# Filter generation and the later modulation products moved from the prologue into the first layer's input projection

## The chip, the cores and the metric

The kernel runs on one core of a Trainium2 chip. The metric is the device time of one execution in microseconds. Three runs of the kernel before gave a median of 3544.75 us (3544.44 to 3552.7). The engines are TensorE (PE; its weight loads are PEld), VectorE (DVE), ScalarE (ACT), GpSimd (POOL) and SyncE (SP, here the queue that issues most transfers).

## The reference

The reference is a two-layer backbone on 1024 latent and 256 context tokens of width 1024. This change touches only what stands before and in the input projection of layer 0:

```python
m_lat = jnp.split((s_lat @ ada_w[i] + ada_b[i])[:, None, :], 6, axis=-1)      # per layer, also with s_ctx
h_lat = modulate(rmsnorm(x_lat, norm1_g[i]), m_lat[0], m_lat[1])              # y * (1 + scale) + shift
u_lat = h_lat @ w_in                                                          # layer 0: 1536 + 384 + 256 + 32 columns

def hyena_filters(L, w1, b1, w2, b2, w3, freq):                               # L = 1024 and 256
    h = jnp.sin(freq * (z @ w1 + b1))
    h = jnp.sin(freq * (h @ w2 + b2))
    h = (h @ w3).reshape(L, HY_ORDER, D_HY)
    return jnp.transpose(h * window[:, None, :], (1, 0, 2))
# later: irfft(rfft(z) * rfft(h)), a long convolution with each of the two filters
```

`ada_w` has 2 x 1024 x 6144 values. Only the first 2048 columns of layer 0 (shift and scale of the first norm) are needed for the first norm.

## The kernel before

The program is a row of blocks; all engines meet at the end of each. The names and lines that matter:

`prologue` loads everything small, `x` (L581) and the constants. It computes the two hidden layers of the filter network (L597, L603) with the sine's argument reduced on VectorE (L650 to L656), the filter tiles of 128 positions by 512 channels (L613, windowed on VectorE at L665), a butterfly of the window's blocks (`butterfly_lat`, `butterfly_ctx`, L451 to L497) and the spectra by matmuls with a table (`forward`, L510 to L516), which ScalarE copies out (L714) and stores. ScalarE squares `x` (L704) and GpSimd adds the squares up in `ss` (L731). Between these, TensorE works through the modulation: class `Stream` loads 32 pieces of `ada_w` of 1.5 MB, each three tiles of 128 columns, into two buffers (L388, L392). For each piece, eight matmuls with 32 stationary columns go to four column groups of the array (L404), ScalarE copies the four partial rows (L421), three matmuls turn and sum them to columns (L410), and ScalarE stores those in `mods` (L424). At the end VectorE makes the coefficients of all four norms (`coefficients`, L433 to L442).

`even_in` begins with the first norm (`Norm`: column sums L307, root and reciprocal, broadcast L315, `rr` L346, `xr` L335, `h_hi` L355, `h_lo` L328) and then multiplies: 18 output tiles ("items") of 128 rows by 1280 tokens, two per weight pair, each with 8 k-tiles x 3 passes (high and low halves of weights and activations) x 3 token chunks. Items 0 and 1 are interleaved (`first_pair`, L273), the rest follow one another (`item`, L252). Per item ScalarE makes the high half of the next weights (L232) and the centre tap of the short convolution or a copy (L772, L785, L787), VectorE the low half (L238) and the outer taps (L802). Two accumulators, banks 0 to 2 and 3 to 5 of PSUM, alternate. The loops over items are hardware loops.

Each engine executes its own queue in order; semaphores order the engines against one another. Nothing else plans the order: it is as written.

Of the kernel before, what the change touches and what calls it, by code (L numbers as in the profile page):

```python
# [29 lines left out]
P = 128  # L30
D = 1024
KT = D // P
# [190 lines left out]
def full(use):  # L223

    return use + 2
# [65 lines left out]
class Norm:  # L291


    def __init__(self, k, n):
# [8 lines left out]
    def tensor(self, k, e):  # L303
        if k.sqs:
            e.wait_ge(k.ss_done, k.sqs)
        for j in range(self.tiles):
            mm = e.matmul(k.bank[:, 6, j:j + 1], k.ss[:, j * P:(j + 1) * P], k.ones[:, 0:1], start=True, stop=True)  # L307
# [11 lines left out]
    def vector(self, k, e):  # L319
        t = self.tiles  # L320
# [3 lines left out]
        e.reciprocal(k.rstd[:, 0:t], k.stat[:, 0:t]).then_inc(k.rstd_ready, 1)  # L324
        e.wait_ge(k.rr_ready, self.bcs + len(self.chunks))
# [14 lines left out]
    def scalar(self, k, e):  # L340
        t, n = self.tiles, self.n
        e.wait_ge(k.ms_ready, n + 1)
        e.activation(k.stat[:, 0:t], k.stat[:, 0:t], ACT.Sqrt).then_inc(k.sd_ready, 1)
        for c, (c0, m) in enumerate(self.chunks):
            e.wait_ge(k.bc_full, self.bcs + c + 1)
            e.activation(self.rr[:, c0:c0 + m], k.bank[:, 7 - c % 2, 0:m], ACT.Copy).then_inc(k.rr_ready, 1)  # L346
        for kk in range(KT):
# [13 lines left out]
ADA_M = 3  # L361
ADA_LOADS = 2 * 48 // ADA_M


class Stream:
# [5 lines left out]
    def __init__(self, k):  # L371
        words = KT * ADA_M * P
        assert H0 + 30080 + ADA_M * P <= END - words and words <= 4 * WS
        self.w = [k.at(f"ada_w{s}", at, [P, KT, ADA_M * P]) for s, at in enumerate((S0, END - words))]
        self.full = [k.sem(f"ada_landed{s}") for s in range(2)]
        self.sums = [k.sem(f"ada_sums{s}") for s in range(2)]
        self.read = [k.sem(f"ada_read{s}") for s in range(2)]
        self.stored = [k.sem(f"ada_stored{s}") for s in range(2)]
        self.columns = [k.sem(f"ada_columns{s}") for s in range(2)]
        self.row = [k.at(f"ada_row{s}", H0 + 28544 + s * ADA_M * P, [P, ADA_M * P]) for s in range(2)]  # L380
        self.group = [[k.bank[32 * j:32 * j + 32, 4 + s, 0:ADA_M * P] for j in range(4)] for s in range(2)]
        self.out = [k.bank[:, 4 + s, 0:ADA_M * P] for s in range(2)]
        self.turned = [k.bank[:, 4 + s, ADA_M * P:ADA_M * (P + 2)] for s in range(2)]
        self.made = self.copied = 0

    def load(self, k, e):
        for s in range(2):
            e.dma_start(self.w[s][:, :, :], k.d["ada_w"][s]).then_inc(self.full[s], 16)  # L388
        with e.Fori(0, ADA_LOADS // 2 - 1) as i:
            for s in range(2):  # L390
                e.wait_ge(self.sums[s], i + 1)
                e.dma_start(self.w[s][:, :, :], k.d["ada_w"][i * 2 + (s + 2)]).then_inc(self.full[s], 16)  # L392

    def products(self, k, e, count):

        with e.Fori(0, count) as n:
            i = n + self.made
            for s in range(2):
                e.wait_ge(self.full[s], i * 16 + 16)
                e.wait_ge(self.stored[s], i + 1)  # L400
                for half in range(2):
                    for j in range(4):
                        kk = 4 * half + j
                        mm = e.matmul(self.group[s][j], k.silu_c[:, 32 * kk:32 * kk + 32], self.w[s][:, kk, :],  # L404
                                      start=(half == 0), stop=(half == 1))
                mm.then_inc(self.sums[s], 1)
            for s in range(2):
# [20 lines left out]
    def coefficients(self, k, e, steps):  # L428
        for s in range(2):
            e.wait_ge(self.stored[s], ADA_LOADS // 2 + 1)  # L430
# [1788 lines left out]
```

## Time and profile before

| | |
|---|---|
| median of three runs | 3544.75 us |
| the profiled execution | 3543.79 us, its span 3542.1 us |
| TensorE busy | 3230.7 us, 91% of the span |
| VectorE, ScalarE, GpSimd busy | 1583.9, 969.9, 357.5 us |
| mean granted TensorE clock | 0.954 |
| loads of `ada_w` | 32 of 1536 KB, all in the first 260 us |
| loads of weight halves | 194 of 512 KB |

A timeline row gives the start, the time, the engine, the line, the operation and its operands, how many instructions are merged in it, and in brackets how long the engine stood before it and what ended that. A float32 matmul appears as two records on TensorE. A row of stretches gives the busy time of each engine in the stretch with its number of instructions, then the granted clock of TensorE (1.00 is 2.4 GHz, 0.50 is 1.2 GHz), the share of the DMA engines and GB/s.

### The profile page before, as it was taken

Reading aid. Unit: us, or ns where it says so; the run is one execution under the profiler, and the core shown is the slowest. Engines: PE = TensorE matmul, PEld = TensorE weight load, DVE = VectorE, ACT = ScalarE, POOL = GpSimd, SP = SyncE. Lnnn points to the kernel's source line nnn. Section 1 sums busy time; section 2 is a strip of 40 time slices with the busy share of each in tenths; the row PEclk is TensorE's granted clock in tenths of the full one; section 3 lists DMA queues with packets and bytes.
Section 4 is the critical chain, followed back from the end, with each engine's and each line's share of the span. In section 5 each row is a group of like instructions: output and inputs, shape, how many; then the busy total and the mean of one; then the engine's idle time right before and its main releaser. Section 6 shows DMA issues by size and latency. Waiting matters only on the chain. (4 is left out here: it accounts for less than half of the span.)

```text
span 3542.1 us, 37967 instructions
## 1 busy us (share of the span) xinstructions
PE 3230.7 (91%) x15170; PEld 2525.1 (71%) x15170; DVE 1583.9 (45%) x1846; ACT 969.9 (27%) x1105; POOL 357.5 (10%) x252
## 2 busy tenths in 40 slices
PE   5878998799965889999999999899988899999999
PEld 2337885455554678888888888777866788888887
DVE  5304316666578533333222322567775432332333
ACT  2224112344410223111111111377782411111111
POOL 3000000177722110000000000200001000000000
PEclk8878999799987999999999999899998999999999
DMA  6772210000211410111111111211103111111112
GB/s 239 284 277 94 80 50 3 0 1 1 116 56 42 154 36 30 36 37 37 41 36 36 39 40 36 80 30 38 36 29 111 49 48 48 47 47 47 47 48 76
DMA packets 45561, 228.95 MB, mean 65 GB/s; under 512 B 6377, under 2 KB 6761, under 8 KB 39179
## 3 DMA queue, kind: packets, MB, share of 16 engines
q1 hardware_dynamic: 41594, 203.37, 16.7%
q10 hardware_dynamic: 1728, 13.63, 0.9%
q0 software_dynamic: 2128, 10.36, 0.7%
q8 instruction: 84, 1.38, 0.2%
q14 instruction: 27, 0.21, 0.0%
HBM read 201.65 MB, written 25.69 MB: 64 GB/s over the span
## 5 line engine op out<-in xcount | busy, mean ns | idle before, releaser
L252 PE MATMUL bank<-h_hi,w_hi 128*128 128x512 f32 (+1 forms) x2616 | 702.7, 368 | 14.1 <-DVE h_lo L1645 7.2
L252 PE MATMUL bank<-h_lo,w_hi 128*128 128x512 f32 (+1 forms) x2616 | 700.5, 368 | 0.0
L252 PE MATMUL bank<-h_hi,w_lo 128*128 128x512 f32 (+1 forms) x2616 | 700.2, 367 | 0.0
L238 DVE TENSOR_TENSOR w_lo<-w_raw,w_hi 128x1024 fp32r<-128x1024 f32 x194 | 262.5, 1353 | 660.9 <-ACT w_hi L232 658.4
L252 PEld LDWEIGHTS bank<-h_hi,w_hi 128*128 128x128 f32 x2616 | 451.9, 188 | 99.5 <-issue 14.6
L252 PEld LDWEIGHTS bank<-h_lo,w_hi 128*128 128x128 f32 x2616 | 452.6, 188 | 88.1 <-issue 2.9
L252 PEld LDWEIGHTS bank<-h_hi,w_lo 128*128 128x128 f32 x2616 | 452.3, 188 | 85.1
L1577 DVE SCALAR_TENSOR_TENSOR x<-bank,c_mods,x 128x1024 f32<-128x1024 f32 (+3 forms) x280 | 271.7, 1005 | 256.5 <-PE bank L252 256.4
L232 ACT ACTIVATE w_hi<-w_raw 128x1024 fp32r<-128x1024 f32 x194 | 203.8, 1051 | 647.7 <-PE bank L252 608.9
L252 PE MATMUL bank<-hid_hi,w_hi 128*128 128x512 f32 (+1 forms) x880 | 242.9, 373 | 11.6 <-DVE x L1577 11.6
L252 PE MATMUL bank<-hid_hi,w_lo 128*128 128x512 f32 (+1 forms) x880 | 240.4, 371 | 0.0
L252 PE MATMUL bank<-hid_lo,w_hi 128*128 128x512 f32 (+1 forms) x880 | 240.4, 371 | 0.0
L1777 DVE TENSOR_TENSOR hid<-silu_gate,bank 128x1280 f32<-128x1280 f32 (+1 forms) x44 | 59.6, 1354 | 393.2 <-PE bank L252 390.8
L1744 ACT ACTIVATE hid_hi<-hid 128x1280 fp32r<-128x1280 f32 (+1 forms) x44 | 51.4, 1167 | 504.7 <-DVE hid L1777 504.7
L252 PEld LDWEIGHTS bank<-hid_hi,w_hi 128*128 128x128 f32 x880 | 153.2, 188 | 47.7 <-DVE x L1577 19.3
L1126 POOL TENSOR_TENSOR a_psum<-a_psum,probsT 128x512 f32<-128x512 f32 x128 | 174.2, 1371 | 28.5 <-ACT probsT L1322 26.9
L252 PEld LDWEIGHTS bank<-hid_hi,w_lo 128*128 128x128 f32 x880 | 154.0, 188 | 29.5
L252 PEld LDWEIGHTS bank<-hid_lo,w_hi 128*128 128x128 f32 x880 | 154.0, 188 | 29.5
L1740 ACT ACTIVATE silu_gate<-bank 128x1280 f32<-128x1280 f32 (+1 forms) x44 | 50.0, 1135 | 422.5 <-PE bank L252 422.5
L1595 POOL TENSOR_TENSOR ss<-ss,sq_ev 128x1280 f32<-128x1280 f32 x14 | 41.4, 2957 | 1027.5 <-ACT sq_ev L1586 1027.4
L1228 DVE TENSOR_REDUCE a_mx<-bank 128x1 fp32r<-128x1280 f32 (+1 forms) x80 | 101.2, 1269 | 90.9 <-PE bank L1141 90.8
L1322 ACT ACTIVATE probsT<-bank 128x512 f32<-128x512 f32 (+1 forms) x176 | 101.8, 578 | 141.7 <-PE bank L1167 138.9
(292 smaller groups left out, 3720.2 us busy)
## 6 DMA issues: line engine op xcount, KB each, us to landing
w_raw<-in_weights SPq DMA_DIRECT2D x194, 512.0 KB, 3.5
ada_w<-in_ada_w SPq DMA_DIRECT2D x32, 1536.0 KB, 7.6
x<-in_x SPq DMA_DIRECT2D x2, 5120.0 KB, 18.4
h_gate<-u_scratch SPq DMA_DIRECT2D x4, 2560.0 KB, 9.5
u_scratch<-uc POOLq DMA_DIRECT2D x12, 640.0 KB, 3.2
spec_lat<-f_spec ACTq DMA_DIRECT2D x2, 3584.0 KB, 10.3
h_spec<-spec_lat SPq DMA_DIRECT2D x2, 3584.0 KB, 12.2
x_kept<-x SPq DMA_DIRECT2D x1, 4096.0 KB, 13.3
```

The costliest lines, as they stand in the source:

```text
L232: e.activation(k.w_hi[s][:, :], k.w[s][:, :], ACT.Copy).then_inc(k.split_hi[s], 1)
L238: e.tensor_tensor(k.w_lo[s][:, :], k.w[s][:, :], k.w_hi[s][:, :].bitcast(F32), ALU.subtract).then_inc(k.split_lo[s], 1)
L252: mm = e.matmul(out[:, c:c + m], w[:, c1:c1 + P], x[:, c:c + m], start=(first and kk == 0 and n == 0), stop=(last and kk == kt - 1 and n = ...
L1126: e.tensor_tensor(part, part, pT[:, u % DEPTH, :], ALU.add).then_inc(sum_done, 1)
L1228: e.reduce_max(mx[:, h % 2, j:j + 1], score_sums(h, j)[:, 0:T if j < 8 else CTX], AX_X).then_inc(mx_done, 1)
L1322: e.activation(pT[:, u % DEPTH, 0:m], k.bank[:, slot_bank(slot), 0:m], ACT.Exp, scale=MLA_SCALE).then_inc(slot_read, 1)
L1577: ins = e.scalar_tensor_tensor(out=k.x[:, m, a:b], in0=k.acc[s][:, a:b], scalar=gate(m, n), in1=old[:, m, a:b], op0=ALU.mult, op1=ALU.add)
L1595: e.tensor_tensor(k.ss[:, 0:tokens], k.ss[:, 0:tokens], sq[:, m % 2, 0:tokens], ALU.add).then_inc(k.ss_done, 1)
L1740: e.activation(sg[:, 0:tokens], k.acc[0][:, 0:tokens], ACT.Silu).then_inc(k.acc_free[0], 1)
L1744: e.activation(hid_hi[buf][:, t, 0:tokens], hid[:, 0:tokens], ACT.Copy).then_inc(hi_done, 1)
L1777: e.tensor_tensor(hid[:, 0:tokens], sg[:, 0:tokens], k.acc[1][:, 0:tokens], ALU.mult).then_inc(hid_ready, 1)
```

## The change

`Stream` now works in 96 tiles of 128 columns (0.5 MB each). The first 16 are loaded at once and computed in the prologue; the other 80 are computed in `even_in`, five in each of the items 2 to 17, behind the k-tiles 0, 2, 4, 5 and 7 (`ADA_STEPS`), with three buffers. A step is: turn the tile before, then the eight products of this one.

The prologue keeps the filter network's hidden layers, now with the 1280 positions as two halves on 128 partitions, and loads `x` before the modulation weights. Squares of `x` have eight buffers and are added by GpSimd (first four) and VectorE (last four). The sums and the root of the first norm, its `rr` and the first weight split come into the prologue; coefficients are made for norm 0 only.

`even_in` is unrolled. The filters are made in four passes (two orders x two halves of 256 channels): filter tiles behind the items 2, 5, 8 and 11, spectra behind the items 4, 7, 10 and 13, both in PSUM banks 6 and 7. Their inputs come on GpSimd's queue, which now also issues the attention's weights only after the last spectra. The coefficients of norms 1 to 3 are made at its end.

```diff
-ADA_M = 3
-ADA_LOADS = 2 * 48 // ADA_M
+ADA_TILES = 2 * 48
+ADA_FIRST = 2 * KT
+ADA_BUFS = 3
...
+    def products(self, k, e, n):
+        late = n - ADA_FIRST
...
+            e.wait_ge(self.late_landed[late % ADA_BUFS], 16 * (late // ADA_BUFS) + 16)
+            e.wait_ge(self.read, n)
+        for half in range(2):
+            for j in range(4):
+                kk = 4 * half + j
+                mm = e.matmul(self.group(k, n, j), k.silu_c[:, 32 * kk:32 * kk + 32], w[:, kk, :],
+                              start=(half == 0), stop=(half == 1))
+        mm.then_inc(self.sums, 1)
...
+    def turn(self, k, e, n):
+
+        e.wait_ge(self.read, n + 1)
+        if n > ADA_FIRST:
+            e.wait_ge(self.stored, n - ADA_FIRST)
+        e.matmul(self.turned(k, n), self.row[n % 2][:, :], k.c["pick"][:, :], start=True, stop=True).then_inc(self.columns, 1)
...
+            for n in range(ADA_FIRST):
+                ada.products(k, e, n)
+                if n:
+                    ada.turn(k, e, n - 1)
+            ada.turn(k, e, ADA_FIRST - 1)
+            e.wait_ge(ones_landed, 32)
+            e.wait_ge(ss_ready, 1)
+            norm.tensor(k, e)
...
+            for n in range(ADA_FIRST):
+                ada.copy(k, e, n)
+            e.wait_ge(ada.columns, ADA_FIRST)
+            e.activation(k.mods[:, 0:2 * ADA_FIRST], k.bank[:, 3, 0:2 * ADA_FIRST], ACT.Copy).then_inc(mods_read, 1)
+            norm.root(k, e)
+            for s in range(2):
+                split_hi(k, e, s, w0, k.acc_full[s], 1)
...
+FILTER_PASSES = [(order, half) for order in range(2) for half in range(2)]
+TILES_AFTER = [2, 5, 8, 11]
+SPECTRA_AFTER = [4, 7, 10, 13]
+ADA_STEPS = (0, 2, 4, 5, 7)
...
+                    if kk == KT - 1:
+                        mm.then_inc(k.acc_full[s], 1)
+                    if kk in ADA_STEPS:
+                        if kk == ADA_STEPS[0]:
+                            filters_read(i)
+                        ada_step(n)
+                        n += 1
...
+            def modulation_read(i):
+                e.wait_ge(ada.read, step_of(i + 1))
+                e.wait_ge(ada.stored, step_of(i + 1) - ADA_FIRST - 1)
+
+            def filter_tiles(p):
+                e.wait_ge(pass_landed, 64 * (p + 1))
+                for m, (first, count) in enumerate(TILES):
+                    if m >= 2:
+                        e.wait_ge(hw_ready, NM * p + m - 1)
...
+            for i in range(2, ITEMS):
+                tile(i)
+                if i in TILES_AFTER:
+                    modulation_read(i)
+                    filter_tiles(TILES_AFTER.index(i))
+                if i in SPECTRA_AFTER:
+                    modulation_read(i)
+                    spectra(SPECTRA_AFTER.index(i))
+            ada.turn(k, e, ADA_TILES - 1)
...
+            for i in range(ITEMS):
+                s, pair = i % 2, i // 2
                 if pair + 1 < ph.pairs:
                     split_hi(k, e, s, w0 + pair + 1, k.acc_full[s], full(a0 + pair))
                 e.wait_ge(k.acc_full[s], full(a0 + pair))
...
+                if 1 <= i < ITEMS - 1:
+                    for n in range(step_of(i + 1), step_of(i + 2)):
+                        if n > ADA_FIRST:
+                            ada.store(k, e, n - 1)
+                        ada.copy(k, e, n)
```

On TensorE's queue, the end of the prologue and the first branch product of `even_in`, before:

```order
L404 MATMUL bank<-ada_w_99,c_silu_c 32x384 x7
L410 MATMUL bank<-c_pick,ada_row_100 128x2 [waits ada_read0]
L410 MATMUL bank<-c_pick,ada_row_100 128x2 x2
L410 MATMUL bank<-c_pick,ada_row_101 128x2 [waits ada_read1]
L410 MATMUL bank<-c_pick,ada_row_101 128x2 x2
L396 REGISTER_ALU
L396 COMPARE_AND_BRANCH
L567 UNCONDITIONAL_BRANCH
L755 UNCONDITIONAL_BRANCH [waits barrier_Pool_Activation_PE_DVE_SP_release]
L307 MATMUL bank<-c_ones,ss 128x1 [waits ss_done]
```

And after:

```order
L429 MATMUL bank<-ada_w_110,c_silu_c 32x128 [waits ada_read]
L429 MATMUL bank<-ada_w_110,c_silu_c 32x128 x7
L438 MATMUL bank<-c_pick,ada_row_114 128x2 [waits ada_read]
L438 MATMUL bank<-c_pick,ada_row_115 128x2 [waits ada_read]
L308 MATMUL bank<-c_ones,ss_first 128x1 [waits x_sum,ones_landed]
L308 MATMUL bank<-c_ones,ss_first 128x1 x9
L316 MATMUL bank<-c_ident,c_rstd 128x128 [waits rstd_ready]
L316 MATMUL bank<-c_ident,c_rstd 128x128 x7
L316 MATMUL bank<-c_ident,c_rstd 128x128 [waits rr_ready]
L316 MATMUL bank<-c_ident,c_rstd 128x128
L590 UNCONDITIONAL_BRANCH
L801 UNCONDITIONAL_BRANCH [waits barrier_Pool_Activation_PE_DVE_SP_release]
```

The norm's column sums follow the 16th modulation tile instead of the 96th, and stand ahead of the block's end instead of behind it.

On the same engine at the seam between two items, before (`w_lo_53` belongs to the item that ends, `w_hi_52` to the next):

```order
L252 MATMUL bank<-h_hi,w_lo_53 128x512 x2
L252 MATMUL bank<-h_hi,w_lo_53 128x256
L252 MATMUL bank<-h_hi,w_hi_52 128x512 [waits sums_read1,weights_lo1]
L252 MATMUL bank<-h_hi,w_hi_52 128x512
L252 MATMUL bank<-h_hi,w_hi_52 128x256
```

And after, behind item 2:

```order
L817 MATMUL bank<-h_hi,w_lo_53 128x256
L438 MATMUL bank<-c_pick,ada_row_115 128x2 [waits ada_stored,ada_read]
L429 MATMUL bank<-ada_late_w_112,c_silu_c 32x128 [waits ada_read,ada_late_landed1]
L429 MATMUL bank<-ada_late_w_112,c_silu_c 32x128 x7
L843 MATMUL bank<-f_w_577,f_sines 128x256 [waits f_pass,ada_stored,ada_read]
L843 MATMUL bank<-f_w_577,f_sines 128x256 x3
L843 MATMUL bank<-f_w_577,f_sines 128x256 [waits f_hw]
L843 MATMUL bank<-f_w_577,f_sines 128x256
L843 MATMUL bank<-f_w_577,f_sines 128x256 [waits f_hw]
L843 MATMUL bank<-f_w_577,f_sines 128x256
L843 MATMUL bank<-f_w_577,f_sines 128x256 [waits f_hw] x2
L817 MATMUL bank<-h_hi,w_hi_52 128x512 [waits sums_read1,weights_lo1]
```

Ten filter matmuls and a modulation step now stand between two items; from the fifth filter matmul on they wait for VectorE (`f_hw`).

## Rows read from the trace of the kernel before

**Rows 1.** Stretches of the span: prologue with the first norm, and the branch products.

```profile
0.00:280.00 280.00, 195.58 (x916) 89.51 (x917) 93.00 (x130) 67.55 (x113) 27.48 (x14) 0.83 0.66 256
280.00:540.00 260.00, 256.02 (x1296) 216.79 (x1296) 83.85 (x82) 58.41 (x53) 9.24 (x17) 0.99 0.20 72
```

**Rows 2.** What TensorE waited for ahead of the modulation products, L404 (us, times).

```profile
  DMA ada_w<-in_ada_w: 58.2, 24
```

**Rows 3.** Timeline at the seam of the blocks, TensorE and VectorE.

```profile
263.55 4.40 PE L307 MATMUL bank<-c_ones,ss 128*128 128x1 f32 x20 [4.58 <-PEq L567]
280.01 1.41 PE L273 MATMUL bank<-h_hi,w_hi 128*128 128x512 f32 x3 [6.68 <-DVE h_lo L328]
262.64 0.17 DVE L441 SCALAR_TENSOR_TENSOR c_coef<-c_mods,c_gains 128x8 f32<-128x8 f32 x1
273.79 2.89 DVE L335 TENSOR_TENSOR xr<-x,rr 128x1280 f32<-128x1280 f32 x2 [5.14 <-ACT rr L346]
```

**Rows 4.** Timeline of the opening: angle steps and squares.

```profile
27.99 2.43 ACT L704 ACTIVATE sq_first<-x 128x1280 f32<-128x1280 f32 x2 [7.91 <-DMA x<-in_x]
28.09 9.66 DVE L654 SCALAR_TENSOR_TENSOR f_arg<-f_tmp,f_arg 64x1280 f32<-64x1280 f32 x3
```

**Rows 5.** Timeline of TensorE: modulation work at either clock level.

```profile
85.63 2.72 PE L410 MATMUL bank<-c_pick,ada_row 128*128 128x2 f32 x12
88.55 2.79 PE L404 MATMUL bank<-ada_w,c_silu_c 128*32 128x384 f32 x16 [0.20 <-DMA ada_w<-in_ada_w]
105.36 2.79 PE L404 MATMUL bank<-ada_w,c_silu_c 128*32 128x384 f32 x32
108.08 1.51 PE L410 MATMUL bank<-c_pick,ada_row 128*128 128x2 f32 x12
109.45 1.10 PE L513 MATMUL bank<-f_xh,f_tab 128*128 128x512 f32 x2
```

**Rows 6.** Timeline behind item 2, ScalarE and VectorE.

```profile
327.84 1.06 ACT L232 ACTIVATE w_hi<-w_raw 128x1024 fp32r<-128x1024 f32 x1 [14.83 <-PE bank L252]
328.80 1.41 ACT L772 ACTIVATE uc<-bank,c_hy_b,c_hy_w 128x1280 f32<-128x1280 f32 x1
328.93 1.23 DVE L238 TENSOR_TENSOR w_lo<-w_raw,w_hi 128x1024 fp32r<-128x1024 f32 x1 [10.53 <-ACT w_hi L232]
330.36 3.75 DVE L802 SCALAR_TENSOR_TENSOR uc<-bank,c_hy_w,uc 128x1023 f32<-128x1023 f32 x4 [0.20 <-ACT uc L772]
```

**Rows 7.** Timeline of the first filter tiles, TensorE and VectorE.

```profile
42.53 17.43 PE L613 MATMUL bank<-f_w,f_tmp 64*128 64x512 f32 x20 [17.82 <-ACT f_tmp L699]
44.71 0.69 DVE L665 TENSOR_TENSOR hw<-bank,window 128x512 f32<-128x512 f32 x1 [3.54 <-PE bank L613]
```

**Rows 8.** Timeline of 256-column float32 matmuls later in the kernel.

```profile
1026.69 0.59 PE L514 MATMUL bank<-h_xh,h_tf 128*128 128x256 f32 x2
1027.12 0.59 PE L515 MATMUL bank<-h_xh,h_tf 128*128 128x256 f32 x2
```

**Rows 9.** Stretches with TensorE's granted clock, the third number from the right.

```profile
130.00:140.00 10.00, 10.00 (x23) 3.73 (x23) 2.76 (x4) 1.30 (x2) 0.00 (x0) 1.00 0.75 321
150.00:160.00 10.00, 6.08 (x41) 2.22 (x41) 10.00 (x18) 0.98 (x2) 0.00 (x0) 0.66 0.82 318
280.00:284.00 4.00, 3.99 (x11) 3.32 (x12) 3.96 (x3) 3.81 (x4) 0.00 (x0) 0.50 0.00 0
300.00:320.00 20.00, 17.04 (x87) 14.22 (x87) 10.61 (x11) 4.74 (x4) 1.09 (x2) 1.00 0.50 188
```

**Rows 10.** Timeline of TensorE: two gaps.

```profile
153.26 1.51 PE L404 MATMUL bank<-ada_w,c_silu_c 128*32 128x384 f32 x8 [4.42 <-DMA ada_w<-in_ada_w]
313.51 0.81 PE L252 MATMUL bank<-h_hi,w_hi 128*128 128x512 f32 x3 [2.96 <-DVE uc L802]
```

**Rows 11.** Timeline at the end of the branch products.

```profile
539.03 1.23 ACT L787 ACTIVATE rope<-bank 32x1280 f32<-32x1280 f32 x1 [12.83 <-PE bank L252]
540.57 4.11 PE L900 MATMUL bank<-wq,lat 128*128 128x384 f32 x12 [1.57 <-PEq L750]
```

More of the change, by code:

```diff
@@ L356, in scalar @@
                          ).then_inc(k.hi_ready, 1)
-ADA_M = 3
-ADA_LOADS = 2 * 48 // ADA_M
+ADA_TILES = 2 * 48
+ADA_FIRST = 2 * KT
+ADA_BUFS = 3
 class Stream:
     def __init__(self, k):
[L372 to L407, printed above, removed]
-                e.wait_ge(self.read[s], i + 1)
-                for m in range(ADA_M):
-                    tr = e.matmul(self.turned[s][:, 2 * m:2 * m + 2], self.row[s][:, m * P:(m + 1) * P],
-                                  k.c["pick"][:, :], start=True, stop=True)
-                tr.then_inc(self.columns[s], 1)
-        self.made += count
-    def copy(self, k, e, count):
-        with e.Fori(0, count) as n:
-            i = n + self.copied
-            for s in range(2):
-                e.wait_ge(self.sums[s], i + 1)
-                e.activation(self.row[s][:, :], self.out[s], ACT.Copy).then_inc(self.read[s], 1)
-            for s in range(2):
-                e.wait_ge(self.columns[s], i + 1)
-                e.activation(k.mods[:, bass.ds(i * (4 * ADA_M) + 2 * ADA_M * s, 2 * ADA_M)], self.turned[s], ACT.Copy
-                             ).then_inc(self.stored[s], 1)
-        self.copied += count
-    def coefficients(self, k, e, steps):
-        for s in range(2):
-            e.wait_ge(self.stored[s], ADA_LOADS // 2 + 1)
@@ L434, in coefficients @@
-        for n in range(4):
+        part = mods[:, first:last, :]
+        bias = k.ada_b[:, first:last].unsqueeze(2).to_broadcast([P, last - first, 2])
+        steps(e.tensor_tensor(part, part, bias, ALU.add))
+        for n in norms:
             gain = k.gains[:, n * KT:(n + 1) * KT]
@@ L779, in _ @@
-            for j in range(LT + 1):
-                s, pair = j % 2, HP + j // 2
+            norm.modulate(k, e)
+            for i in range(ITEMS):
+                s, pair = i % 2, i // 2
                 if pair + 1 < ph.pairs:
@@ L799, in _ @@
+            norm.apply(k, e)
+            for i in range(ITEMS):
+                s, pair = i % 2, i // 2
+                if pair + 1 < ph.pairs:
+                    split_lo(k, e, s, w0 + pair + 1)
+                if i < CONV:
+                    e.wait_ge(centre, i + 1)
                     n = 0
```

468 lines of the change are left out of this document (276 added, 192 removed).

## The prediction

> **What bounds the kernel now.** I read the stretches of the span first, then the timeline of TensorE at the seam between the prologue and `even_in`, then the waits of the modulation products. The prologue and the first norm take 280.0 us, in which TensorE is busy 195.6 us and the DMA queues move 256 GB/s; in `even_in` (280 to 540) TensorE is busy 256.0 of 260 us [rows 1]. So there are two kinds of time here: before 280 it is the stream of 48 MB of `ada_w` that sets the pace (TensorE waited 58.2 us for it in 24 waits [rows 2]), and after 280 every microsecond that is added to TensorE's queue is a microsecond of the span. The change takes 80 of 96 modulation tiles and all filter work after the angle reduction out of the first kind of time and puts them into the second. The question is whether 202 us won in the prologue pay for that.
>
> **When the first branch product starts.** Before, the norm's sums start at 263.55, `xr` at 273.79 and the first product at 280.01 [rows 3]. After, step by step:
> - `x` lands. Before, ScalarE waited for it until 27.99 [rows 4], behind about 2.9 MB of window and other inputs; 8.1 MB in the 21.5 us since its issue are 0.38 MB/us, so 5.24 MB alone land at about 20.
> - ScalarE then does four squares, the second sine and four squares; two squares took 2.43 us [rows 4]. The second sine waits for the angle: its three long steps took 9.66 us on 1280 columns beside GpSimd's adds [rows 4]; on 640 columns that is 4.8 us, so the angle is ready at 27.7. The squares end at 33.4, the logarithm with its table at 34.9. ScalarE is in order, so the first modulation row is copied only then.
> - 16 modulation tiles in series. At the low clock level (0.50, 1.2 GHz) 16 records of 384 columns took 2.79 us and 12 turning records 2.72 us [rows 5]; with a third of the columns that is 1.1 + 0.45 + 0.15 for changing the array's shape = 1.7 us per tile; at the high level 1.0 (next part). About 7 us low and the rest high: 35 + 21 = 56 (53 to 62). The 8.4 MB of these tiles land at about 42 and are not late.
> - The norm then needs 10.2 us to `xr` (263.55 to 273.79 [rows 3]), so its `rr` is there at 66. But now the two weight splits stand behind `root` on ScalarE: 2 x 1.06 us and one 1.23 us on VectorE after them [rows 6], then 8 small operations of about 0.2 us (one took 0.17 [rows 3]) and a block end of 0.6. `xr` starts at 71.9, and 6.2 us later [rows 3] the first product: **78 us** (70 to 85). That is 202.0 us earlier.
>
> **The modulation steps in `even_in`: 80 of them.** Each is one turning matmul (2 records) and 8 products (16 records). At the high level 12 turning records take 1.51 us less overlap, from 108.08 to the next at 109.45 = 0.114 each, so 0.23. 32 records of 384 columns take 2.72 us (105.36 to 108.08), of which 8 groups of four at once x 0.32 us are columns; the rest, 0.14, and 0.1 on the way in are the change of shape [rows 5]. With 128 columns 4 groups x 0.11 = 0.44. Sum 0.23 + 0.44 + 0.3 (in and out, after a turning matmul that must end first) = 1.0 us; x 80 = **+80 us**. Lower bound 0.69 each without any price of the change (55 us); upper bound if a record cannot start faster than the 0.085 us that these rows show: 16 x 0.085 + 0.35 = 1.71 (137 us). I take 1.0, since 384 columns fill the 0.085. The waits in these steps (`ada_read`, `ada_stored`, landing) are for things two or more microseconds old. A load is issued when the tile three before it is done, at least 9 us ahead.
> These rows do not exclude that the sequencer is the limit. The Trainium skill, "TensorE: Matmul & The Clock Gate", section "Wait — 56ns, not 53.3ns?", gives about 62 ns of sequencer time per matmul where it decodes them itself; an estimate by that page is 16 x 0.062 = 0.99 us instead of 0.44, +44 us over 80 steps, and a time of 3593. The trace's smallest spacing, 0.085, is above it and cannot decide.
>
> **The filter tiles: 4 passes.** Call E the end of an item's products (`acc_full`). Before, ScalarE's split starts at E (327.84), its centre tap at +1.0, VectorE's split at +1.1, and the taps end at +6.3 [rows 6]. Now the last modulation step keeps ScalarE until E + 1.4, so the taps end at E + 7.7. TensorE writes the first two filter tiles (two 256-column matmuls each) at once and then stands: the third needs a bank that VectorE reads only behind the taps (0.69 us for 512 columns [rows 7]). So TensorE idles from about E + 3.2 to E + 8.6. What follows a gap of this size is in the trace: after 4.42 us without work [rows 10] the next 10 us had 0.66 mean clock [rows 9], the 2.96 us gap before 313.51 [rows 10] lies in a stretch of 1.00, and dense products that began at the low level stood at 0.50 for 4 us [rows 9] (by 286 they had the full rate). So the other four tiles run at the low level (20 records of 512 columns took 17.43 us there [rows 7], so a 256-column matmul of two records takes 0.87 there, twice the 0.43 of rows 8) and end at E + 13.5, and the next item loses 2.4 us of its first 4.8. Less the 0.95 us of the modulation step already counted: 13.5 - 0.95 + 2.4 = 14.95, x 4 = **+60 us** (44 if the clock stays up, 68 if it comes back later). VectorE's butterflies behind it lie beside the next item: VectorE is busy 83.9 of 260 us in this block [rows 1], and all filter work adds some 17 us in each of four places.
>
> **The spectra: 4 passes.** 30 matmuls of 256 columns at 0.43 us [rows 8] are 12.9 us. They start at E + 1.5, and the third group waits for ScalarE, which first does its split and centre tap (to E + 3.9) and then a 512-column copy of 0.6: 1.4 us of standing, too short for the clock. They end at E + 15.8, less 0.95: 14.85 x 4 = **+59 us**. Before, the same matmuls stood in the prologue beside the stream.
>
> **The end of `even_in`.** Before, the `rope` copy at 539.03 was followed by the next block at 540.57 [rows 11]. Now the last turning matmul, its store, and 14 operations of 0.2 us on VectorE stand there: +5 us, and TensorE, idle for over 5 us, starts `latents` at the low level: +2.5. **+7.5 us** (3 to 9). The taps, splits, `u` stores and weight loads keep their order and their slack.
>
> **The sum.** -202.0 + 80 + 60 + 59 + 7.5 = +4.5 us against the profiled execution's 3543.8, so 3548.3; the median shown is 1.0 above it: **3549 us**. Everything after `even_in` is untouched.
>
> **Rivals.**
> - *The clock does not fall* (0.22). The third filter tile waits, but the modulation steps around it keep the level: -16 us in the filters, -5 in the prologue, which runs its 16 tiles at the high level. 3528 us. For it: the second filter stage of before, at 130 to 140, kept 1.00 throughout [rows 9]. Against it: the 4.42 us gap.
> - *The modulation steps are issue bound* (0.20, slower). Place: 16 records per step, 80 times on the path; price: up to 0.7 us each, 57 us: 3606 us. From 0.08 us over my 1.0 the kernel is measurably slower, so this decides soon. For it: the trace has no row with more than 12 records a microsecond. Against it: the columns explain that row.
> - *The modulation tiles are late* (0.12). Three buffers and a queue shared with weights, window and spectra: before, TensorE waited 2.4 us each of 24 times [rows 2]. 1 us in each of 16 items: 3565 us. Against it: 0.5 MB in at least 9 us is 58 GB/s, a fifth of what the prologue moved.
> - The forecast itself has 0.46.
>
> **The numbers.** A measurement of this kernel can tell about 0.3%, 10.6 us, from no change. Faster: the first rival, 0.22. Within: 0.46. Slower: the other two, 0.32. The range reaches from the first rival's time to 3572, which takes in the late tiles, 15 us of errors in the start of the first product and in the filters' stalls, and the lower half of what the issue could cost; beyond it lie the full price of the issue and a clock that stays up with every term low.
>
> **What would show it.** In the profile of the changed kernel: the first L273 product at 78 us; `ada_late_w` groups of 16 records about 0.5 us long with 1.0 us between the products around them (1.4 or more: the issue rival); in each of four places a TensorE gap of 5 to 6 us ended by VectorE's `f_hw` and a granted clock under 1.00 behind it; spectra of 14 us without a fall; `latents` starting at about 543. I am wrong in the main thing if the items with five steps take other than 19.1 us, or if the product starts before 70 or after 85.

## The result, and the profile after

The changed kernel takes **3527.89 us** (median of 4 runs, 3527.11 to 3528.97), the kernel before in the same comparison 3547.64 (4 runs, 3544.44 to 3552.7): ratio of the runs as recorded 0.9941, 95% interval 0.9929 to 0.9953 (the two medians alone give 0.9944). It is 0.6% faster, where the forecast was no measurable change (3549). The medians differ by 19.8 us. The profiled executions, on which the accounts below are made, have spans of 3526.2 and 3542.1 us, a difference of 15.9.

The stretches of the changed kernel, in the columns of [rows 1] (TensorE's busy time first, then its loads, VectorE, ScalarE, GpSimd, granted clock, DMA share, GB/s); the block of the branch products now ends at 523:

```profile
0.00:76.00 76.00, 37.87 (x344) 27.81 (x344) 27.29 (x35) 30.30 (x47) 10.26 (x8) 0.94 0.56 214
76.00:523.00 447.00, 409.71 (x3056) 333.95 (x3056) 149.15 (x253) 112.73 (x250) 20.11 (x34) 0.94 0.51 174
```

The prologue shrank from 280 to 76 us and the block behind it grew from 260 to 447, of which TensorE stands still for 37 (447.0 less 409.7). What it waits for in that block (total us, times, longest) names the places; 4.7 us more stand at the block's end:

```profile
PE bank L843 <- DVE f_hw L938: 23.2, 8, 5.6
PE bank L541 <- ACT f_spec L898: 2.8, 4, 0.7
PE bank L817 <- DVE uc L923: 2.8, 1, 2.8
PE bank L538 <- ACT ada_row L444: 1.6, 4, 0.4
```

L843 is a filter tile, L817 a branch product, L538 and L541 are spectra. No row of the block's waits names a DMA: the later modulation tiles are never late.

The seam between the blocks (timeline; answers to [rows 3], where the norm's sums, `xr` and the first product are at 263.55, 273.79 and 280.01):

```profile
32.44 0.59 PE L438 MATMUL bank<-c_pick,ada_row 128*128 128x2 f32 x2 [4.63 <-ACT ada_row L444]
32.96 1.08 PE L429 MATMUL bank<-ada_w,c_silu_c 128*32 128x128 f32 x16
...
54.73 4.41 PE L308 MATMUL bank<-c_ones,ss_first 128*128 128x1 f32 x20
70.17 2.90 DVE L342 TENSOR_TENSOR xr<-x,rr 128x1280 f32<-128x1280 f32 x2 [0.53 <-PEq L590]
76.40 1.19 PE L273 MATMUL bank<-h_hi,w_hi 128*128 128x512 f32 x2 [12.07 <-DVE h_lo L335]
```

A tile of the prologue is one such turn and 16 records. From one turn to the next it is 1.53 us, the same for all tiles, up to the norm's sums at 54.73.

A modulation step between branch products, and the start of filter pass 0 behind item 2 with its gap, on TensorE:

```profile
122.81 0.28 PE L438 MATMUL bank<-c_pick,ada_row 128*128 128x2 f32 x2
123.02 0.65 PE L429 MATMUL bank<-ada_late_w,c_silu_c 128*32 128x128 f32 x16
123.59 0.85 PE L817 MATMUL bank<-h_hi,w_hi 128*128 128x512 f32 x3
124.27 0.76 PE L817 MATMUL bank<-h_lo,w_hi 128*128 128x512 f32 x3
...
128.46 1.14 PE L843 MATMUL bank<-f_w,f_sines 64*128 64x256 f32 x8 [0.40 <-ACT ada_row L444]
135.23 2.67 PE L843 MATMUL bank<-f_w,f_sines 64*128 64x256 f32 x8 [5.62 <-DVE f_hw L938]
138.09 1.82 PE L843 MATMUL bank<-f_w,f_sines 64*128 64x256 f32 x4 [0.19 <-DVE f_hw L938]
139.83 1.43 PE L817 MATMUL bank<-h_hi,w_hi 128*128 128x512 f32 x3
141.06 1.27 PE L817 MATMUL bank<-h_lo,w_hi 128*128 128x512 f32 x3
```

The step reads: turn 0.21 (122.81 to 123.02), products 0.57 (to 123.59), and the first branch pass behind it takes 0.68 to the next instead of 0.59: 0.87 us in all. In the pass, eight records took 1.14 us ahead of the gap and 2.67 behind it, and the next item opens with 1.23 us a branch pass instead of 0.59. VectorE in that gap has its split and taps, and then the windowing that TensorE waits for:

```profile
130.70 3.64 DVE L923 SCALAR_TENSOR_TENSOR uc<-bank,c_hy_w,uc 128x1023 f32<-128x1023 f32 x4
134.48 1.29 DVE L938 TENSOR_TENSOR f_hw<-bank,f_window 128x512 f32<-128x512 f32 x2
```

The granted clock (third number from the right) ahead of the gap, in it, and behind it; it falls in the same way in all four passes:

```profile
119.00:129.00 10.00, 9.60 (x94) 7.87 (x93) 0.00 (x0) 1.94 (x7) 0.00 (x0) 1.00 0.40 131
129.00:135.00 6.00, 0.60 (x6) 0.20 (x2) 5.27 (x6) 1.67 (x2) 0.31 (x1) 0.77 0.25 87
135.00:139.00 4.00, 3.58 (x11) 2.57 (x12) 2.06 (x4) 0.00 (x0) 0.22 (x1) 0.50 0.41 164
```

The last four items have no filter work. They begin at 443.54 and end with the products of 517.08 (0.57 more):

```profile
443.54 0.93 PE L817 MATMUL bank<-h_hi,w_hi 128*128 128x512 f32 x3
...
517.08 0.65 PE L429 MATMUL bank<-ada_late_w,c_silu_c 128*32 128x128 f32 x16
...
523.16 6.60 PE L1025 MATMUL bank<-wq,lat 128*128 128x384 f32 x12 [4.66 <-PEq L760]
```

74.1 us for four is 18.5 each. An item without steps is 14.1 (before, 225.5 us for 16), so a step costs 4.42 / 5 = **0.884 us**.

**The account**, forecast against measured, in us:

| term | forecast | measured | how measured |
|---|---|---|---|
| first branch product | -202.0 | -203.6 | 280.01 to 76.40 |
| 80 modulation steps | +80 | +70.7 | 80 x 0.884 |
| filter tiles, 4 passes | +60 | +54.2 | items 11.7 to 11.9 longer than clean ones, the next ones 1.2 to 2.2 |
| spectra, 4 passes | +59 | +57.6 | items 14.4 longer, the last 14.3 |
| end of `even_in` | +7.5 | +5.8 | 5.5 us instead of 1.7 from the last item's end to the next block, and 2.0 more in `latents` |
| rest | 0 | -0.6 | difference |
| sum | +4.5 | -15.9 | spans |

### The profile page after: what moved, and what is told of

It reads as the page before. It is cut to its first block and busy times, and to the rows that moved or that the text cites. A ratio compares the mean times of both kernels' runs of the same rounds, so it can differ in the third digit from the quotient of the medians.

```text
span 3526.2 us, 40361 instructions
## 1 busy us (share of the span) xinstructions
PE 3230.3 (92%) x16358; PEld 2583.3 (73%) x16358; DVE 1584.1 (45%) x1922; ACT 986.8 (28%) x1236; POOL 350.9 (10%) x263
## 5 line engine op out<-in xcount | busy, mean ns | idle before, releaser
L252 PE MATMUL bank<-h_hi,w_hi 128*128 128x512 f32 (+1 forms) x2232 | 606.2, 370 | 9.2 <-DVE h_lo L1770 7.2
L252 PE MATMUL bank<-h_lo,w_hi 128*128 128x512 f32 (+1 forms) x2232 | 604.7, 369 | 0.0
L252 PE MATMUL bank<-h_hi,w_lo 128*128 128x512 f32 (+1 forms) x2232 | 604.5, 369 | 0.0
L252 PEld LDWEIGHTS bank<-h_hi,w_hi 128*128 128x128 f32 x2232 | 388.2, 188 | 85.2 <-issue 11.6
L252 PEld LDWEIGHTS bank<-h_lo,w_hi 128*128 128x128 f32 x2232 | 388.8, 188 | 73.9
L252 PEld LDWEIGHTS bank<-h_hi,w_lo 128*128 128x128 f32 x2232 | 388.4, 188 | 73.9
L1902 DVE TENSOR_TENSOR hid<-ss_first,bank 128x1280 f32<-128x1280 f32 (+1 forms) x44 | 59.6, 1355 | 393.2 <-PE bank L252 390.7
L1865 ACT ACTIVATE ss_first<-bank 128x1280 f32<-128x1280 f32 (+1 forms) x44 | 50.0, 1135 | 420.0 <-PE bank L252 420.0
```

Source lines behind the costliest of these rows:

```text
L252: mm = e.matmul(out[:, c:c + m], w[:, c1:c1 + P], x[:, c:c + m], start=(first and kk == 0 and n == 0), stop=(last and kk == kt - 1 and n = ...
L1865: e.activation(sg[:, 0:tokens], k.acc[0][:, 0:tokens], ACT.Silu).then_inc(k.acc_free[0], 1)
L1902: e.tensor_tensor(hid[:, 0:tokens], sg[:, 0:tokens], k.acc[1][:, 0:tokens], ALU.mult).then_inc(hid_ready, 1)
```

## The experiments

Eleven kernels were run. Where nothing else is said, a time is one run with its profile, to be held against the span of 3526.2. The changed kernel itself was not run again beside them, and the kernel before took 3549.9 to 3553.5 us there instead of 3547.64, so a few us in the whole time show nothing. The first branch product and the start of `latents` in each trace split a difference by place, and so do the items (from the start of one item's products to the next): they repeat to about 0.1 us where the clock stays up. From the first branch product to `latents` the changed kernel takes 446.8 us.

**Without the later modulation.** The loads, products, turns, copies and waits of the 80 later tiles are left out, and zeros stand in the place of what they give.

```diff
-                        ada_step(n)
-                        n += 1
...
-            ada.turn(k, e, ADA_TILES - 1)
```

> The changed kernel without its 80 modulation steps in even_in (the modulation of the later norms and gates is left out, zeros in its place). Theory: a step costs what the array needs, 0.88 us by the spacing of the items 14 to 16 in the profile after (18.51 us against 24 x 0.587 = 14.09), and all of it is on the path: items of 14.1 us, span 3526.2 - 70.7 = about 3455.5, with the four stalls for the windowed filter tiles 0.5 to 1 us shorter each. Rival: part of the steps stands in time that the items would spend otherwise (weights, taps), so that fewer than 60 us go and items stay above 14.5.

Measured 3451.93, span 3450.1: -76.1. Clean items (those without filter work) are 14.08 us instead of 18.51, so the steps' own 70.7 are confirmed. The way from the first product to `latents` is 72.8 us shorter: beside the steps 3.8 are the gap at the block's end, which is 1.7 us again, and 0.7 the first pair, while the filter passes with the items behind them take 2.6 us more. 3.6 us are behind `latents`' start (2994.7 us from there to the last matmul instead of 2998.3). VectorE's gaps in the filter passes grew, from 23.2 to 24.6 us, so the expected shorter stalls did not come:

```profile
PE bank L837 <- DVE f_hw L927: 24.6, 8, 6.0
```

**What a step is made of.** The eight products twice, and the turn twice.

```diff
-        for half in range(2):
+        for half in [0, 1] * (1 if late < 0 else 2):
```

> The changed kernel with the eight products of each of the 80 steps made twice in a row (same result). Theory (the array's columns are the price): 4 groups of 0.112 us more per step, 0.45 x 80 = 36 us, span about 3562. Rival (the issue of 16 more records is the price, 0.06 us each or more): 0.99 us a step, 79 us, span about 3605. This tells which of my two sizes of the step was wrong, the products or the change of shape.

```diff
-        e.matmul(self.turned(k, n), self.row[n % 2][:, :], k.c["pick"][:, :], start=True, stop=True).then_inc(self.columns, 1)
+        for again in range(1 if n < ADA_FIRST else 2):
+            mm = e.matmul(self.turned(k, n), self.row[n % 2][:, :], k.c["pick"][:, :], start=True, stop=True)
+        mm.then_inc(self.columns, 1)
```

> The changed kernel with each of the 80 turning matmuls in even_in made twice (same result). Theory: 2 records at 0.112 us more, 0.22 x 80 = 18 us, span about 3544; then the rest of the step's 0.88 us, 0.88 - 0.45 - 0.22 = 0.21, is the change of shape, which I had priced at 0.3. Rival: the turning matmul is paid as latency ahead of the products, which it makes wait for its end, and a second one hides in it: less than 8 us.

Measured spans 3562.3 (+36.1, 0.45 a step) and 3545.4 (+19.2, 0.24 a step, against a rival of less than 8 us). By clean items, 20.71 and 19.65 us instead of 18.51, it is 0.44 and 0.23 a step. One step of the first, on TensorE:

```profile
123.80 1.08 PE L429 MATMUL bank<-ada_late_w,c_silu_c 128*32 128x128 f32 x32
...
```

32 records last 1.01 us (123.80 to the branch product at 124.81), 16 last 0.57: 16 more cost 0.44, 28 ns each. The issue rival, which needed up to 85 ns a record, is refuted, and the forecast's 0.44 for the products and 0.23 for the turn are exact. What is left of 0.884 for the shape change is 0.2 (0.21 by the items, 0.19 by the spans), where the forecast had 0.3.

**The shape change by itself.**

```diff
+                        if p == 1 and kk in ADA_STEPS:
+                            if kk == ADA_STEPS[0]:
+                                filters_read(i)
+                            ada_step(n)
...
-                        ada_step(n)
+                        ada.products(k, e, n, (1,))
```

(`ada_step` here makes the turn and the first four products only.)

> Each later modulation step is cut in two: its turn and the first four products stand ahead of the last pass of the contraction tile, the other four behind it, so that TensorE goes from 128x128 to 128x32 and back twice a step, with the same number of products and turns. Theory (of the 0.88 us of a step 0.45 are the eight products, 0.24 the turn and 0.19 the change of shape in and out): 80 more changes of 0.19, 15 us, span 3541. The prediction's price of a change, 0.3, would give 24 us, 3550. Rival (the remainder of 0.19 is the wait between turn and products or a wait for a modulation copy, not the shape): within 3 us of 3526.2, or less than before.

Measured 3556.92, span 3555.1: +28.9, 0.36 for each added change. But 4.3 us of that are item 2 alone (34.50 instead of 30.18 us), where every clean item grew by 1.60, to 20.11. By the clean items an added change is 0.32: over half as much again as the theory's 0.19, and close to the forecast's 0.3. The rows show how 0.32 here goes with 0.2 in a step:

```profile
123.70 0.28 PE L439 MATMUL bank<-c_pick,ada_row 128*128 128x2 f32 x2
123.91 0.43 PE L429 MATMUL bank<-ada_late_w,c_silu_c 128*32 128x128 f32 x8
124.26 0.85 PE L818 MATMUL bank<-h_hi,w_lo 128*128 128x512 f32 x3
125.04 0.42 PE L429 MATMUL bank<-ada_late_w,c_silu_c 128*32 128x128 f32 x8
125.40 0.84 PE L818 MATMUL bank<-h_hi,w_hi 128*128 128x512 f32 x3
...
```

Four products take 0.35 us where four more behind them would take 0.22, so 0.13 are paid on entering; a branch pass behind products takes 0.1 more than 0.59 (125.40 to the next at 126.08), and one that also has products behind it another 0.1 (124.26 to 125.04 is 0.78). Entering from a wide pass and returning costs 0.13 + 0.1 + 0.1 = 0.33, as the items say. Entering from the turn costs 0.13 + 0.1 = 0.23: the 0.1 that a wide pass pays ahead of products is not there. The theory that a change costs the same wherever it stands falls; that the remainder of a step is the change of shape stands.

**The gap in the filter passes.** 48 products of 128x256 that nothing reads stand in it.

```diff
+                    if m == 2:
+                        other = (TILES_AFTER[p] + 1) % 2
+                        e.wait_ge(k.acc_free[other], a0 + (TILES_AFTER[p] + 1) // 2 + 1)
+                        for _ in range(48):
+                            e.matmul(k.bank[:, 3 * other + 2, 256:512], k.h_hi[:, 0, 0:P], k.h_hi[:, 0, 0:256], start=True, stop=True)
```

> The changed kernel with 48 float32r matmuls of 256 columns into unused PSUM columns between the second and the third filter tile of each pass (extra work without a result), which fill the 5.6 us in which TensorE waits for VectorE. Theory (the gap lets the clock fall, and that costs beside the gap): granted clock 1.00 over the passes, the tiles behind the gap and the item after them at full rate; 1.4 us less in the tiles and 1.2 to 2.2 us less in the next item per pass, 10 to 14 us in all, span 3512 to 3516. Rival (the clock falls for another reason, or the gap itself is the whole price): span 3526 or more.

Measured 3513.61, span 3511.8: -14.4. The next tile comes no earlier than before (7.0 us behind the first, against 6.8), but the clock stays up:

```profile
128.93 6.01 PE L842 MATMUL bank<-h_hi 128*128 128x256 f32 x48
134.87 1.48 PE L848 MATMUL bank<-f_w,f_sines 64*128 64x256 f32 x8
...
138.00 0.85 PE L817 MATMUL bank<-h_hi,w_hi 128*128 128x512 f32 x3
```

The pass is 10.1 us instead of 11.4 (127.86 to 138.00, 128.46 to 139.83), and the next item opens at the full rate and takes 18.50 us, a clean item's time, in all four places. The four passes with the items behind them are 11.7 us shorter; the other 2.7 of the 14.4 lie elsewhere, 2.1 of them behind `latents`' start. So of a pass's 13.55 us, 2.9 are the lower clock behind the gap.

**No gap: the tiles elsewhere.**

```diff
+                    if kk == 3 and i - 1 in TILES_AFTER:
+                        modulation_read(n)
+                        filter_tiles(TILES_AFTER.index(i - 1))
...
-                if i in TILES_AFTER:
-                    modulation_read(i)
-                    filter_tiles(TILES_AFTER.index(i))
```

> The filter tiles of a pass stand behind contraction tile 3 of the next item instead of behind the whole item, so that VectorE has finished its taps when they are issued. Theory (a pass costs 13.55 us because the engine stands still 5.6 us behind VectorE's taps and then runs at the lower clock into the next item): without the gap the clock stays up, a pass costs what its products and VectorE's five windowings take, 5 to 6 us; 4 x 8 to 8.5 us less, the span falls by 30 to 38 us, to about 3492. Rival (a pass is bound by VectorE's chain of windowings and what stood behind the gap only moves): the gap goes, 4 x 5, but the clock still falls somewhere inside the item: about 3505 to 3512.

Measured 3495.91, span 3494.1: -32.1, inside the theory's interval and outside the rival's; from the first product to `latents` it is 32.5 us less. A pass takes 5.04 us, and its item 23.75, 5.2 more than a clean one:

```profile
138.03 1.14 PE L848 MATMUL bank<-f_w,f_sines 64*128 64x256 f32 x8
139.94 1.72 PE L848 MATMUL bank<-f_w,f_sines 64*128 64x256 f32 x8 [0.77 <-DVE f_hw L940]
141.84 1.30 PE L848 MATMUL bank<-f_w,f_sines 64*128 64x256 f32 x4 [0.18 <-DVE f_hw L940]
143.07 0.85 PE L817 MATMUL bank<-h_hi,w_hi 128*128 128x512 f32 x3
```

**The spectra elsewhere.** As above, behind contraction tile 1 (`kk == 1`), with ScalarE's copies moved behind the copy of that item's first modulation tile.

```diff
+                    if kk == 1 and i - 1 in SPECTRA_AFTER:
+                        modulation_read(n)
+                        spectra(SPECTRA_AFTER.index(i - 1))
```

> The 16 spectra of a pass stand behind contraction tile 1 of the next item, and ScalarE's copies of them behind the copy of that item's first modulation tile. Theory (of the 14.4 us of a set 13 are ScalarE's and TensorE's alternation, and 1.5 are the wait for the last modulation copy and for VectorE's or ScalarE's work on the item just ended): 4 x 1 to 1.5 us less, span about 3521. Rival (the alternation is all, wherever the set stands): within 1 us of 3526.

Measured 3521.12, span 3519.3: -6.9. The sets take 12.94 to 13.0 us instead of 13.8 to 14.0, back to back at 0.43 us a product as the forecast's 12.9 said, and the wait of 0.40 ahead of them is gone. That accounts for 5.4, inside the theory's 4 to 6. The rest stands behind the second and the fourth filter pass: the items there took 19.8 and 19.9 us instead of 20.7, in code that is the same.

**The prologue: splits in the norm's shadow.**

```diff
-            norm.invert(k, e)
             for s in range(2):
                 split_lo(k, e, s, w0)
             e.wait_ge(others, 16 * len(names))
             e.wait_ge(mods_read, 1)
+            norm.invert(k, e)
...
-            norm.root(k, e)
             for s in range(2):
                 split_hi(k, e, s, w0, k.acc_full[s], 1)
+            norm.root(k, e)
```

> In the prologue both splits of the first weights stand ahead of the norm's root and of its inverse, and the coefficients directly behind the inverse. Theory (the 5.5 us between the last copy of rr and the first product of x and rr are VectorE's splits and coefficients, and all of it fits beside the broadcast): the first branch product comes 4.5 to 5.3 us earlier, at 71.1 to 71.9 instead of 76.40; the span is 3521.3. Rival (TensorE's or the barrier's time decides, as the broadcast would start later behind the splits on ScalarE): 0 to 2 us.

The first branch product came at 71.32, 5.1 us earlier, as the theory had it. The span fell by only 0.8, to 3525.4 (3527.15 measured) and not to the theory's 3521.3; by the whole time the rival's 0 to 2 us would fit as well, and only the place speaks for the theory. 1.4 of the missing 4.3 us are between the first product and `latents` (448.1 instead of 446.8), in the first pair and item 2; 2.9 are behind `latents`' start, in code that is the same. One such place, first in the changed kernel, then in this one:

```profile
2252.59 0.85 PE L252 MATMUL bank<-hid_hi,w_hi 128*128 128x512 f32 x3 [1.81 <-DVE x L1702]
...
2254.45 0.75 PE L252 MATMUL bank<-hid_hi,w_hi 128*128 128x512 f32 x3
```

```profile
2250.09 0.85 PE L252 MATMUL bank<-hid_hi,w_hi 128*128 128x512 f32 x3 [1.81 <-DVE x L1702]
...
2252.24 1.27 PE L252 MATMUL bank<-hid_hi,w_hi 128*128 128x512 f32 x3
```

The same wait of 1.81 us at the same instruction left the rate alone in one execution and halved it for some 3 us in the other. Over all kernels here the time from `latents`' start to the last matmul is 2994.7 to 3001.1 us, so a gain of a few us at one place may be swallowed by that, in either direction.

**The prologue: dense work ahead of the tiles.**

```diff
             e.wait_ge(silu_ready, 1)
+            for _ in range(16):
+                e.matmul(k.bank[:, 7, 0:256], k.silu_c[:, 0:P], k.silu_c[:, 0:256], start=True, stop=True)
             for n in range(ADA_FIRST):
                 ada.products(k, e, n)
+                if n == 1:
+                    for _ in range(10):
+                        e.matmul(k.bank[:, 7, 0:256], k.silu_c[:, 0:P], k.silu_c[:, 0:256], start=True, stop=True)
```

> 16 products of silu_c with itself (128x256, float32) stand ahead of the first modulation tile and 10 more ahead of its turn, in a bank that nothing reads. Theory (the 16 tiles run at the lower clock because TensorE was nearly idle before them, and with dense work ahead the engine has the higher one when they begin and keeps it): a tile takes about 0.9 instead of 1.53 us, the norm's 40 products 0.11 instead of 0.22 us each; the first branch product comes 10 to 14 us earlier, at 62 to 67; the span is about 3514. Rival (the tiles themselves, 32 columns wide products and turns, do not hold the higher clock, whatever stood before): 0 to 4 us less, tiles of 1.53 us again after the first few.

Measured 3524.1, span 3522.3; the first branch product at 70.79, 5.6 us earlier, between theory and rival. A tile takes 0.89 us until TensorE waits 1.0 us for weights, and 1.53 behind that:

```profile
40.65 0.64 PE L429 MATMUL bank<-ada_w,c_silu_c 128*32 128x128 f32 x16
42.61 0.90 PE L429 MATMUL bank<-ada_w,c_silu_c 128*32 128x128 f32 x16 [1.00 <-DMA ada_w<-in_ada_w]
43.95 1.08 PE L429 MATMUL bank<-ada_w,c_silu_c 128*32 128x128 f32 x16
```

So the tiles hold the higher level for 9 us if they begin at it, which they don't reach by themselves in 22. Of the 5.6 us, 1.6 are lost again ahead of `latents`, in the first pair and item 2, as in the kernel above.

**All together.** Both moves in `even_in`, both edits of the prologue, and three filling products ahead of tile 12, where the wait was:

```diff
             for n in range(ADA_FIRST):
+                if n == 12:
+                    for _ in range(3):
+                        e.matmul(k.bank[:, 7, 0:256], k.silu_c[:, 0:P], k.silu_c[:, 0:256], start=True, stop=True)
                 ada.products(k, e, n)
```

> Filter tiles behind contraction tile 3 and spectra behind contraction tile 1 of the next item, both splits ahead of the norm, the filling products ahead of the first modulation tile and of its turn, and 3 more ahead of tile 12, which waits for its weights. Theory (the parts touch different stretches and add up): -32.1 - 6.9 for filters and spectra; the first branch product at 59 to 64 instead of 76.4, if the higher clock now lasts through the tiles and the norm, of which 2 are lost again in the first pair; the span is 3526.2 - 39 - 11 to 15, 3472 to 3476. Rival (the two moves in even_in get in each other's way on ScalarE, and the level falls in the norm): 3480 to 3490.

Measured **3479.02** (5 runs, 3476.47 to 3483.18; the kernel before 3549.9, 9 runs): ratio to the kernel before 0.9794, interval 0.9781 to 0.9808. The first branch product is at 63.12, and the tiles keep their rate past the filling:

```profile
41.77 1.54 PE L635 MATMUL bank<-c_silu_c 128*128 128x256 f32 x6
43.24 0.64 PE L429 MATMUL bank<-ada_w,c_silu_c 128*32 128x128 f32 x16
47.19 2.37 PE L308 MATMUL bank<-c_ones,ss_first 128*128 128x1 f32 x20
51.53 4.64 PE L316 MATMUL bank<-c_ident,c_rstd 128*128 128x128 f32 x20 [1.97 <-DVE c_rstd L329]
```

From the first product to `latents` it takes 413.8 us, 33 less than the changed kernel; the two moves alone gave 32.5 and 6.8, so 6 us of their sum are missing. Filter passes are 5.05 to 5.57 us here and spectra 12.94 to 13.0, so they keep most of their gains; but behind the first pass the lower rate shows again, for 3 us:

```profile
128.32 1.43 PE L825 MATMUL bank<-h_hi,w_hi 128*128 128x512 f32 x3
```

The items that hold the first three filter passes (3, 6 and 9) take 25.25, 25.27 and 26.66 us, where the fourth, and all four with the tiles moved alone, take 23.75: these are 5.9 of the 6 us. The clock fell in each of the three. Why it did here, behind waits no longer than 0.8 us, no run shows. The profiled execution was the slowest of the five (span 3481.3); the median run has a span of 3477.2, 1 us above the theory's 3472 to 3476 and below the rival's 3480 to 3490. Against the changed kernel it is 49 us less, where the four parts alone were 32.1, 6.9, 0.8 and 3.9.

**The norm's gap filled too.** The kernel with all parts, and eleven filling products ahead of the first branch product.

```diff
+            for _ in range(11):
+                e.matmul(k.bank[:, 5, 0:256], k.silu_c[:, 0:P], k.silu_c[:, 0:256], start=True, stop=True)
             first_pair(k, e, w0, a0, k.rhs_h, (T, T), k.h_ready, norm.h_base)
```

> As the kernel with all parts together, and 11 more filling products between the norm's last product and the first branch product. Theory (the first pair begins at the lower clock because TensorE stands still for 7 us before it, which costs 2 us): 1.5 to 2.5 us less than together. Rival (the fillings run at the lower clock, 0.85 us each, and the first product waits for them): 2 to 3 us more.

Measured 3478.8, span 3477.0, 4.3 less than the profiled execution of the kernel above, but its time is about that kernel's median: by the whole time nothing is shown. By place: the first product comes 0.3 earlier and opens at the full rate, where it was at half:

```profile
62.81 0.81 PE L273 MATMUL bank<-h_hi,w_hi 128*128 128x512 f32 x3 [1.25 <-DVE h_lo L335]
```

Yet the way to `latents` is only 0.4 us shorter (413.4), and 3.6 of the difference lie behind it, so what the first pair won (31.15 us instead of 32.73) was given back in the items behind it: item 2 took 21.08 us instead of 18.33, item 3 23.75 instead of 25.25. The theory holds for the first pair and not for the whole.

## Why the prediction was wrong

**Where it was right.** The shape of the account: some 200 us out, some 190 in, and the terms' order. The first product was forecast at 78 and came at 76.40, through the chain that was named (squares, logarithm, tiles, norm, splits, coefficients). The filter gap of 5 to 6 us ended by `f_hw` is there at 5.62, with the granted clock at 0.50 behind it; no modulation tile is late. The spectra take their 14 us, but stand 0.7 us for ScalarE's copies and not 1.4, and 0.4 ahead of the first.

**The step that failed** is "0.23 + 0.44 + 0.3 (in and out, after a turning matmul that must end first) = 1.0 us; x 80 = +80 us". A step costs 0.884. The mechanism (all of a step is on the path, and it is made of records, a turn and a change of shape) is right, and turn and products are as forecast; the size of the change of shape is not. Its 0.3 had a surcharge for the turn ahead of the products, and the turn does the reverse: behind it the change costs 0.2, and 0.32 where the products stand directly behind a wide pass. The terms add up to 0.97, which was then rounded to 1.0; that alone is 2.4 us of the 80 steps. The text named 19.1 us for an item as its test; 18.5 came. 0.12 us is little, but multiplied by 80 it gives 9.3 of the 20.4 us of error, and the time came out just under the range's lower end of 3528. (The lower bound of 0.69 is 0.67 by its own terms.)

**The other sizes.** The filter passes are 5.8 us below +60: a pass made its item 11.7 to 11.9 us longer, not 12.55, and the next item lost 1.2 to 2.2 us, 1.7 in the mean, not 2.4. The gap had about its forecast length (5.6 us against 5.4) and ended 8.0 us after the item's products, not 8.6. First product -1.6, spectra -1.4, end -1.7, rest -0.6. All six differences go the same way. For the steps (0.97 to 1.0) and for the prologue's tiles (below) the prediction's own terms show a rounding towards the dearer side; for the others that is a guess. In a sum of six terms such roundings are a bias, not a safety margin.

**The first product was right by two errors.** "About 7 us low and the rest high: 35 + 21 = 56" failed: all 16 tiles ran at 1.53 us, the low rate, to 54.7. They took 22.6 us from the first copied row (32.1) to the norm's sums, where the forecast had 21. But the chain began 2.8 us earlier (32.1 against 34.9), since the second sine came at 25.33, and the two errors nearly cancel. Two sums in that step are off: a third of 2.79 us is 0.93, not 1.1, and with it a tile at the low rate is 1.53 us, as measured, and not 1.7; and 7 us low with the other tiles at 1.0 are 19 us, not 21.

**The rivals.** The first, "the clock does not fall", has 3528 us, the time that was measured, and is still refuted: the clock fell in all four passes, and the prologue's tiles ran at the low rate. With the clock kept, the filled gap shows 3513.6, with 11.7 us less at the passes. That the rival's total came true is chance: a matching total is no evidence for a mechanism. The issue rival is refuted by the products made twice (28 ns a record), the late tiles by the missing DMA row among the waits. The Trainium skill, "TensorE: Matmul & The Clock Gate", section "Wait — 56ns, not 53.3ns?", gives about 62 ns per matmul for a sequencer that decodes them itself, and the prediction's estimate counted that once for each record. The doubled products cost 28 ns a record, 55 ns for the two records of a matmul, so the 44 us of that estimate did not come, and the measurement decides; whether the sequencer decodes here is not shown by any run.

**What it meant for the change.** The change works, but gives back on the path 54 us of filters and 58 of spectra that the prologue had beside its stream. Most of a pass's 13.55 us was a matter of place: the same tiles four contraction tiles later cost 5.0 to 5.2, and that is most of the way from 3528 to 3479.

## What to carry to other kernels

Work that is moved between dense products should stand where the engine that consumes it is already free, not at the end of an item, where that engine has its own work. Here the wait was paid once in time (5.6 us) and again in the clock (2.9). A unit cost that is multiplied by 80 should be composed from its parts (records, turn, shape) with the neighbours that it will really have, and unknowns should be taken at their middle, since cautious roundings add up. And when a change wins a few us in one stage, read that stage, since the same code elsewhere moved by up to 6 us here.

## What the runs showed that was not expected

- **A granted clock of 1.00 stands over work at the low rate.** The tiles of the prologue, at 1.53 us each, and the same tiles at 0.89 us, in the kernel with all parts together, both have 1.00. The first level that the trace of the changed kernel records stands at 64.0 us, in the other kernel at 18.9, so the first of these rows rests on no record:

```profile
30.00:55.00 25.00, 22.56 (x258) 16.45 (x258) 7.52 (x4) 6.51 (x20) 3.22 (x1) 1.00 0.61 221
```

```profile
32.00:49.00 17.00, 16.27 (x279) 12.76 (x279) 6.25 (x4) 6.28 (x21) 1.46 (x1) 1.00 0.78 279
```

  So in a kernel's opening the level is to be read from the duration of a known record (16 records at 1.08 or 0.64 us), not from that column. The row of 1.00 at 130 to 140 in [rows 9], on which the first rival leaned, is not of that kind: behind 62.9 us the kernel before has recorded levels, and the 20 records that took 17.43 us in [rows 7] last 9.60 there:

```profile
135.07 9.60 PE L613 MATMUL bank<-f_w,f_tmp 64*128 64x512 f32 x20
```

- **22 us of unbroken work stayed at 1.2 GHz.** From 32.4 to 54.7 TensorE had no pause that the trace shows, at the low rate throughout. Dense 128x256 products ahead took it to the rate of 2.4 GHz, and the same tiles then held it for 9 us, and with three fillings over the wait up to the norm, 15 us.
- **Leaving a wide product directly for 32-column ones costs 0.32 us in and out; by way of a turn 0.2.**
- **The same 1.81 us wait can end the higher level or not**, with nothing different at the place itself. What decides it stays open. The items behind the four filter passes, which alternate between 19.7 and 20.7 us, may be a case of the same.
